# Two projection parts at a time by seven half-size products (Strassen's form) in a one-core decoder mixer layer

## The reference

```python
    h = _rmsnorm(x, g_pre) * (1 + scale[:, None]) + shift[:, None]
    p = h @ w_in
    hc, bc, cc, gc, q, k, v, ga = jnp.split(p, _split_points(), axis=-1)
    u = cc * hc
    conv_y = sum(conv_w[i] * u_pad[:, i:i + L] for i in range(CONV_WIDTH))
    ya = _rmsnorm(bc * conv_y, g_conv) * jax.nn.silu(gc)
    o = attend(q, k, v, b_sb).reshape(Bsz, L, ATT_DIM)
    yb = _rmsnorm(o, g_attn) * jax.nn.silu(ga)
    m = jnp.concatenate([ya, yb], axis=-1) @ w_out
    y = x + gate[:, None] * _rmsnorm(m, g_post)
```

## Time and profile before

| | |
|---|---|
| median of 3 runs | 873.62 us (872.91 to 875.14) |
| profiled execution, its own time | 872.5 us |
| its span in the trace | 870.7 us |
| PE busy | 825.4 us (95%) |
| DVE, POOL, ACT busy | 526.9, 376.9, 348.9 us |
| granted TensorE clock, mean | 0.989 of full speed |
| moved | 191 MB, 220 GB/s over the span |

### The profile page before, as it was taken

How to read it: one execution, slowest core, us unless ns; L and a number is a source line. 1 busy time by engine, 2 the same in 40 slices (tenths; PEclk the granted TensorE clock), 3 DMA queues, 4 the chain that set the end, 5 groups by cost and what they waited for, 6 DMA issues and landing times.

```text
span 870.7 us, 15500 instructions
## 1 busy us (share of the span) xinstructions
PE 825.4 (95%) x4267; PEld 488.4 (56%) x4267; DVE 526.9 (61%) x691; ACT 348.9 (40%) x682; POOL 376.9 (43%) x186
## 2 busy tenths in 40 slices
PE   0899989999999999999999999999999999899996
PEld 0455756555667565565765655658555555344442
DVE  2554678676584767737857768287686774223334
ACT  6311057574112575811136666211565741111222
POOL 0006782653677355525865455268446430100000
PEclk9989999999999999999999999999999999999998
DMA  8997685576788866657888675687986757373101
GB/s 320 331 309 254 219 268 168 170 226 207 234 253 270 276 208 215 222 172 252 270 271 261 223 244 177 200 256 252 282 249 212 238 185 302 106 236 100 71 24 51
DMA packets 129221, 191.25 MB, mean 220 GB/s; under 512 B 9817, under 2 KB 50822, under 8 KB 129121
## 3 DMA queue, kind: packets, MB, share of 16 engines
q1 hardware_dynamic: 97920, 174.38, 60.9%
q10 hardware_dynamic: 31200, 15.73, 6.4%
HBM read 181.58 MB, written 8.51 MB: 218 GB/s over the span
## 4 chain that ended last, share of the span: by engine, by line
PE 88%; DVE 3%; issue 2%; SPq 2%; DMA 2%; ACT 1%; POOL 1%; POOLq 0%; DVEq 0%; ACTq 0%
PE ps L1144 83%; PE ps L1300 4%; DMA pages<-in_page_table_dram 1%; PE ps L1185 1%; SPq L319 1%; POOL prod L539 1%; DMA hT<-in_w_out_dram 1%; DVE xy L851 1%; DVE ps L1024 0%; DMA ring<-in_cache_v_dram 0%; PE ps L1327 0%; SPq L359 0%; SPq L351 0%; DVE zc L1030 0%; ACT gcb L572 0%
## 5 line engine op out<-in xcount | busy, mean ns | idle before, releaser
L1144 PE MATMUL ps<-hT,wsl 128*128 128x344 f32 x1344 | 425.3, 458 | 3.5 <-issue 3.5
L539 POOL TENSOR_TENSOR prod<-ring,qb 128x1024 f32<-128x1024 f32 x128 | 313.2, 2470 | 220.3 <-DMA ring<-in_cache_k_dram 93.9
L1144 PEld LDWEIGHTS ps<-hT,wsl 128*128 128x128 f32 x1344 | 241.6, 190 | 156.7 <-issue 43.0
L1000 DVE TENSOR_REDUCE zd<-prod 128x16 f32<-128x1024 f32 x128 | 154.1, 1213 | 37.1 <-POOL prod L539 35.9
L1010 DVE TENSOR_SCALAR zc<-ps,bsb 128x512 f32<-128x512 f32 (+3 forms) x96 | 55.5, 613 | 70.3 <-PE ps L1144 68.9
L1144 PE MATMUL ps<-ring,apad 128*8 128x512 f32 (+1 forms) x608 | 82.9, 626 | 2.5 <-DMA ring<-in_cache_v_dram 2.2
L572 ACT ACTIVATE av<-ps 128x512 f32<-128x512 f32 (+3 forms) x96 | 46.7, 487 | 86.2 <-PE ps L1300 85.4
L1144 PE MATMUL ps<-hT,xy 128*128 128x512 f32 x160 | 72.1, 594 | 0.5 <-DMA hT<-in_w_out_dram 0.5
L1024 DVE TENSOR_TENSOR_SCAN ps<-rise,ps 128x512 f32<-128x512 f32 (+3 forms) x64 | 65.6, 1025 | 9.8 <-ACT ps L572 8.7
L1144 PEld LDWEIGHTS ps<-wsl,hT 128*128 128x128 f32 (+1 forms) x576 | 63.5, 181 | 6.2 <-ACT vN L572 2.6
L1144 PE MATMUL ps<-wsl,hT 128*128 128x128 f32 (+1 forms) x576 | 66.5, 275 | 0.0
(11 more groups left out here) (210 smaller groups left out, 662.6 us busy)
## 6 DMA issues: line engine op xcount, KB each, us to landing
ring<-in_cache_k_dram SPq DMA_DIRECT2D x256, 256.0 KB, 3.0
ring<-in_cache_v_dram SPq DMA_DIRECT2D x256, 256.0 KB, 3.0
wsl<-in_w_in_dram ACTq DMA_DIRECT2D x30, 512.0 KB, 5.7
ring<-in_w_ada_dram SPq DMA_DIRECT2D x6, 2048.0 KB, 11.3
xy<-in_x_prompt_dram SPq DMA_DIRECT2D x2, 2048.0 KB, 10.4
out_dram<-oT SPq DMA_DIRECT2D x8, 512.0 KB, 4.0
ring<-in_x_prompt_dram SPq DMA_DIRECT2D x8, 512.0 KB, 6.5
hT<-in_w_out_dram SPq DMA_DIRECT2D x5, 512.0 KB, 5.6
```

The lines of the kernel that those rows point to most:

```text
L539: pool.tensor_tensor(prod[:, p % 2].rearrange("p (j c) -> p j c", j=2), kring[:, p % 4], qb[:, p // 16].unsqueeze(1).to_broadcast([P, 2, H ...
L1000: v.tensor_reduce(zd[:, t // 16, :, r:r + 2], prod[:, t % 2].rearrange("p (j h d) -> p h j d", j=2, h=NH), AX_X, ALU.add)\
L1144: return nc.tensor.matmul(out, l, r, start=start, stop=stop, skip_group_check=True)
```

## The change

Two parts A (two blocks of 128 output channels) and the tokens B are cut in half along channels and tokens. Their product is made by seven products of half size in place of eight, in Winograd's form of Strassen's scheme. There are three pairs of parts (Q,K), (GC,GA), (HC,CC); in group 0 Q and K stay as they were, V and BC stay everywhere. So 11 pairs change.

- `channel_sums` on DVE makes T1 to T4, sums and differences of the quarters of `hT` (128x2064 each), once, in slot 0 of group 0, behind `gates(0)`. They take the room of `xy`, and more.
- `weight_sum` on POOL makes S1, S2, S4 and one sum in place (128x512 each) for each pair: 44 instructions. For (Q,K) of the next group they stand at the end of a group, for (GC,GA) in slots 7 and 8, for (HC,CC) in slots 17 to 20.
- `product(i, j)` on PE is half product `j` of half pair `i`: 4 matmuls with 258 moving tokens. Seven of them make 258 tokens of one half and 258 of the other, for both parts; two half pairs make a pair. They use three banks BX, BV, BY. ACT copies product 1 into BY (`st_seed`), so that BY can be added to, and copies out P5, U2 (`stage`), C11 and C21; DVE adds C12 and C22 (`product_sum`).
- Product 2 waits for `st_seed`, 3 for ACT's copy of P5, 7 for ACT's copy of U2, 4 for DVE's `product_sum(..., 7)`. In groups 1 to 3 the first of these sums stand in DVE's slots 3 and 6.
- The gated parts of groups 0 to 2 are written to DRAM (`y_parts`) in slot 6 of the next group and read back before the output projection (6 loads of 512 KB). The row `gp` goes the same way.
- `sp` has one buffer in place of two and `av` three in place of four. The silu steps on ACT and POOL are moved some slots later. `key_rows` uses the bank OB and stands a slot later. The decode sums use BX and BV.

```diff
-PJ = 24
+PJ = 6
...
-KS = ((range(0, 1), range(1, 2)), (range(2, 6), range(6, 8)))
+HB = NT // 2
+SC = HB // 2
+SLABS = ((0, 1), (0, 3), (1, 2))
+
+PIECES = {"open": (((0, 1, range(0, 2)),), ((0, 1, range(2, 4)),), ((0, 5, range(0, 2)),), ((0, 5, range(2, 4)),)),
+          "mid": (((0, 2, range(0, 1)),), ((0, 2, range(1, 2)),), ((0, 2, range(2, 4)), (0, 6, range(0, 2))), ((0, 6, range(2, 4)),)),
+          0: (((-1, 4, range(0, 1)),), ((-1, 4, range(1, 2)),), ((-1, 4, range(2, 4)), (0, 1, range(0, 4))), ((0, 5, range(0, 2)),)),
+          1: (((0, 5, range(2, 3)),), ((0, 5, range(3, 4)),), ((0, 2, range(0, 4)), (0, 6, range(0, 2))), ((0, 6, range(2, 4)),)),
+          2: (((0, 3, range(0, 1)),), ((0, 3, range(1, 2)),), ((0, 3, range(2, 4)), (0, 7, range(0, 2))), ((0, 7, range(2, 4)),))}
+
+EARLY = ((1, 5), (2, 6), (3, 7, 11), (4, 15), (12, 16), (13, 17))
...
+        T1, T2, T3, T4 = [xT4[:, 4 * HB * i:4 * HB * (i + 1)].rearrange("p (k c) -> p k c", k=4) for i in range(4)]
+        S1, S2, S4 = [wS[:, i, :].rearrange("p (k c) -> p k c", k=4) for i in range(3)]
...
+        BX, BV, BY = PJB, PJB + 1, MB
+        BANK = {1: BX, 2: BX, 5: BV, 3: BV, 6: BY, 7: BY, 4: BY}
...
@@ SP @@
+                    if not first and t == 6:
+                        for b, src in enumerate((gcb, gab)):
+                            sp_e.wait_ge(part_ready, 2 * g)
+                            sp_e.dma_start(y_parts[b][bass.ds(g - 1, 1)].rearrange("a p s -> (a p) s"), src[:, 0:SEQ])\
+                                .then_inc(part_out, 16)
...
+            sp_e.wait_ge(part_out, 32 * (GROUPS - 1))
+            sp_e.wait_ge(st_full[4], 6 * GROUPS - 2)
+            for k in range(GROUPS - 1):
+                for b in range(2):
+                    sp_e.dma_start(yT[:, GROUPS * b + k, :], y_parts[b, k]).then_inc(part_in, 16)
...
@@ POOL @@
+                    if t == 7:
+                        weight_sum(g, 1, 0)
+                        weight_sum(g, 1, 1)
+                    if t == 8:
+                        weight_sum(g, 1, 2)
+                        weight_sum(g, 1, 3)
+                    if t in (17, 18, 19, 20):
+                        weight_sum(g, 2, t - 17)
...
@@ ACT @@
-                    if t in (15, 25):
-                        silu_step(g, t // 25, 0)
-                    if t in (17, 27):
-                        silu_step(g, t // 27, 1)
-                        silu_step(g, t // 27, 2)
+                    if t in (21, 27):
+                        silu_step(g, t // 27, 0)
+                    if t in (23, 29):
+                        silu_step(g, t // 29, 1)
+                        silu_step(g, t // 29, 2)
...
@@ DVE @@
+            def channel_sums():
+                b11, b12 = hT[:, 0:4, 0:HB], hT[:, 0:4, HB:NT]
+                b21, b22 = hT[:, 4:8, 0:HB], hT[:, 4:8, HB:NT]
+                v.wait_ge(h_ready, 1 + 3 * KT)
+                v.tensor_tensor(T1, b12, b11, ALU.subtract).then_inc(t_sum, 1)
+                v.tensor_tensor(T3, b22, b12, ALU.subtract).then_inc(t_sum, 1)
+                v.wait_ge(t_sum, 2)
+                v.tensor_tensor(T2, b22, T1, ALU.subtract).then_inc(t_sum, 1)
+                v.wait_ge(t_sum, 3)
+                v.tensor_tensor(T4, b21, T2, ALU.subtract).then_inc(t_sum, 1)
...
+                    if not first and t in (3, 6):
+                        product_sum(g, first, t // 6, 3)
+                        product_sum(g, first, t // 6, 7)
+                    if u > 0 and u % 6 == 0:
+                        product_sum(g, first, 1 + u // 6, 3)
+                        product_sum(g, first, 1 + u // 6, 7)
...
                     if first and t in (0, 5):
                         gates(t // 5)
+                    if first and t == 0:
+                        channel_sums()
...
@@ PE @@
+                        if j == 2:
+                            pe.wait_ge(st_seed, n + 1)
...
+                        if j == 3:
+                            pe.wait_ge(e_p5, n + 1)
...
+                        if j == 7:
+                            pe.wait_ge(e_u2, n + 1)
+                        if j == 4:
+                            pe.wait_ge(d_c22, n + 1)
```

More of the change, by code:

```diff
@@ L96, in pairs_at, with pieces_at @@
     return (16 + late.index(slot),) if slot in late else ()
+def pieces_at(u):
+    i = u // 2
+    step, chunk = ("open", "mid")[i] if i < 2 else i % 3, 2 + i // 3
+    return [[(chunk + back, j, ks) for back, j, ks in piece] for piece in PIECES[step][2 * (u % 2):2 * (u % 2) + 2]]
 def quad_of(slot):
@@ L609, in _ @@
             act.wait_ge(qs_ps, 1)
[L610 removed]
+            run(qsP, ps[:, DB, :], ACT.Copy, qs_copied, scale=HD ** -0.5)
             act.wait_ge(qs_ps, 2)
@@ L640, in evac, with evac_v @@
+            def evac_v(g, first, c):
+                act.wait_ge(pj_full, PJ * g + c + 1)
+                src = ps[:, PJB + c % 2, :]
+                if c < 2:
+                    if c == 0 and not first:
                         act.wait_ge(vout, 16 * g)
-                    run(vN[:, 4 * (m - 6):4 * (m - 5), :], src.rearrange("p (t c) -> p t c", t=4), ACT.Copy, pj_free)
-                elif m == 8:
+                    run(vN[:, 4 * c:4 * (c + 1), :], src.rearrange("p (t c) -> p t c", t=4), ACT.Copy, pj_free)
+                else:
+                    load_w(g, CC_, 2)
@@ L713, in weights @@
                 act.wait_ge(lwT_full, NU * g + u + 1)
-                if not (first and u < 4):
-                    act.wait_ge(pv_done, NU * g + u - 3)
-                run(av[:, u % 4, 0:P * UNITS[u][2]], ps[:, Z + u % 3, 0:P * UNITS[u][2]], ACT.Exp, a_ready)
+                if not (first and u < 3):
+                    act.wait_ge(pv_done, NU * g + u - 2)
+                run(av[:, u % 3, 0:P * UNITS[u][2]], ps[:, Z + u % 3, 0:P * UNITS[u][2]], ACT.Exp, a_ready)
             def body(g, first, last):
@@ L745, in body @@
                     if t >= 8 and t < SLOTS and u % 2 == 1:
-                        evac(g, first, last, 9 + u // 2)
+                        i = u // 2
+                        for back, j in {0: ((-1, 4), (0, 1)), 1: ((0, 5), (0, 2), (0, 6)), 2: ()}[i % 3]:
+                            if i or not back:
+                                evac_st(g, first, last, 2 + i // 3 + back, j)
                     if first and t in (1, 5):
@@ L1040, in _ @@
             for step in range(6):
-                gating(GROUPS - 1, step)
+                gating(GROUPS - 1, step, True)
             links[0] = 0
```

431 lines of the change are left out of this document (321 added, 110 removed).

## The result

The changed kernel takes **897.02 us** (median of 4 runs, 895.36 to 898.62), the kernel before 873.31 beside it: 1.027 times as long (95% interval 1.024 to 1.029), 23.7 us slower. The forecast was 877.1 us with a range of 861 to 889.

A forecast was written before the change was run, and what follows sets the result against it. PE, busy 95% of the span, was taken to bound the kernel. 872.5 - 35.4 + 9.1 + 16.6 + 9.0 + 4.2 = 876.0 us profiled; the median is 1.1 higher, so 877.1 us, range 861 to 889.

The forecast's parts named there:

- Two times at which PE could reach product 4: Groups 2 and 3: PE could be at product 4 at 408.2 and 575.9, ahead of DVE's sums.
- the part of the forecast that was counted as slower: Forecast's own range, 869 to 885, had chance 0.48; just over half of it counted as slower, above 876.2.
- Fewer products, -35.4: PE's products: 56 matmuls of 444 ns replace 48 of 585 ns, 3.2 us less for each of 11 pairs, -35.4 us.
- rival C: PE's short matmuls don't keep pace: 490 ns a half product matmul and not 444, 905 us; chance 0.05.
- Group 0, +9.1: Channel sums in DVE's queue delay `gates(1)` and `turn(0)` by 8.2 us; 0.85 us of saving lost: +9.1 us.
- Product 4 waits for DVE, +16.6: Start of groups 1 to 3: PE waits 4.0, 5.8 and 6.8 us for DVE sums behind gating step 2, +16.6.
- rival B: DVE late a second time, at the second pair of product sums: 4.0 us in each of three groups, 889.1; chance 0.17.
- Attention units, +9.0: Between `scores` and `turn`, cover shrinks 0.85 us at units 0, 2, 4, 10, 16, 22; waits sum to +9.0 us.
- Rival A: At `turn` of units 0, 2, 16, 22 the units don't wait: 868.1 us without those 9.0; chance 0.30.
- POOL: "The others stand in slots where POOL has time", 0: POOL's weight sums, 1.3 us each, other than (Q,K)'s four: hidden where POOL has time, adding nothing.
- The clock, +4.2: After new PE waits a clock drop costs 1.7 us: half for group 1, one each for groups 2 and 3.
- Transfers, 0: Reading parts back from DRAM needs 11 us, covered by PE's work before the output projection: nothing, at most 2 us.

The follow-up runs named there:

- Runs 5: Changed kernel with DVE's four channel sums ahead of `gates(0)` in place of behind it: 885.92 us, 1.012 of the kernel before.
- 6: Kernel before with four additions of 128x2048 on DVE behind `gates(0)` in group 0, into a tile nobody reads: 882.76 us, 1.010.
- Run 7: Changed kernel with DVE's two product sums of the first half pair ahead of gating step 2 in place of behind it: 892.96 us, 1.021.
- run 12: Changed kernel with later reductions, early channel and product sums, spread read-back, and groups written out in place of the loop: 857.42 us, 0.982 of the kernel before.
- Runs 1: Changed kernel with POOL's (GC,GA) weight sums in slot 6 in groups 1 to 3, in slots 6, 9 and 10 in group 0: 884.31 us, 1.010.
- 2: Changed kernel with DVE's reductions of slots 9 to 31 one slot later, behind the next scan: 883.05 us, 1.009 of the kernel before.
- 3: Kernel before with four sums of 128x512 on POOL in slots 7 and 8 of each group, into a tile nobody reads: 883.28 us, 1.008.
- run 4: Changed kernel without the writes of the gated parts to DRAM and without their read-back: 886.61 us, 1.015 of the kernel before.

## Why the prediction was wrong

Its sum ran to 876.0 for the profiled execution; 898.6 came. The table of stretches splits the 22.6 us: 5 of work, 6 to 7 of idle, 11 of half clock. The sum itself is added up rightly. Two times at which PE could reach product 4 are 0.1 us too late (408.1 and 575.8), and the part of the forecast that was counted as slower, 0.23 of 0.48, is just under half of it and not just over.

- **Fewer products, -35.4: the work fell by 30.** The rival C (490 ns in place of 444) is false, but the price was a little low. Rows of half products with nothing between start 1.74 us apart, 435 ns a matmul, and 1.83 to 1.85 next to other work, as ahead of the last row here (after, group 3):

```profile
582.41 1.90 PE L1348 MATMUL ps<-xT,wS 128*128 128x258 f32 x8
584.15 1.90 PE L1348 MATMUL ps<-hT,wsl 128*128 128x258 f32 x8
585.89 1.90 PE L1348 MATMUL ps<-xT,wS 128*128 128x258 f32 x8
587.73 1.06 PE L1348 MATMUL ps<-ring,apad 128*8 128x512 f32 x8
```

  The cleanest measure is the pair of kernels written out: 165.9 and 157.9 us of work in a group with three pairs, so 2.7 us a pair and not 3.2. 144 matmuls of 585 ns less 8.0 us, over 168 matmuls, is 454 ns. The line through 128 and 344 columns gave 444 ns, 2% high for a steady row and 2% low for the mean. The mean has 42 short sequences a group in it, where there were 18; that their starts make the difference fits the 0.1 us at each, but no run shows it alone.
- **Group 0, +9.1: right.** The wait is 9.31 us, 8.5 more than before, and the sums take 2.3 us each (2.4 estimated). Runs 5 and 6 show the cause. The 2.08 us wait at `turn(0)` is one of 2.07 at `turn(1)` now. The text took the half clock behind the gates to be hidden, and it wasn't: from 110.4 to 115.0 the clock was 0.50 with PE busy throughout, 2.3 us, and a wait of 0.76 for POOL's first weight sum followed.
- **Product 4 waits for DVE, +16.6: right in kind and place, 13.2 in size.** 2.48, 3.82 + 1.10 and 5.78 against 4.0, 5.8 and 6.8. In group 2 product 2 waited for ACT first, as written, and inside the same 5 us. Run 7 shows the cause: step 2. Of that step's 4.9 us in group 3 the scan and the copy of two columns take 3.3, held by POOL's products (run 12), as they were before (3.7). The second pair of sums was waited for nowhere, so rival B didn't come.
- **Attention units, +9.0: mostly false.** Unit 22 waits 0.63, 0.63 and 0.47 us in groups 1 to 3, unit 16 about 0.2, unit 0 not at all: with units 1 and 6 some 3.9 us in the whole kernel, 0.6 before, `turn(2)` and group 0's `turn(1)` left aside, which belong to other terms. Rival A had this right. What is free at a unit can't be read off as the time from the subtraction to the transpose alone; once something upstream is late, DVE and ACT wait less for PE (this is argued; no run isolates it).
- **POOL: "The others stand in slots where POOL has time", 0. This is the step that failed.** Pair 17 came late behind the four sums of (GC,GA): 13.7 us at `turn(2)` in four groups, some 2 of it by the writes, and 8.1 us of half clock behind: together 21.8 us in this profile, where the miss is 22.6, and the other terms, some over and some under, come to about 1 us. Runs 1 and 2 give back 14 to 16 us of it, since other waits take a part of the place. The text took care of (Q,K)'s sums and of the tiles' due times, and called POOL's slots 7 and 8 free because POOL waits there. But POOL's waits in those slots are for keys and for DVE, and five microseconds of sums ahead of pair 17 aren't hidden by a wait that comes before pair 14. The prediction asked for the channel sums who stands behind them in the queue; asked here, the same question finds DVE's reduction of pair 17, which needs POOL's product, and behind it the scan of unit 2. Runs 1, 2 and 3 show it.
- **The clock, +4.2: 15.5.** Not the price of a drop (1.7 us for 3.4 us at half speed) was off but the number: seven stretches at 0.50 in the groups, where two and a half were priced, in two of them PE was busy 4.7 and 6.0 us and not 3.2 to 3.4, and one more in the output projection. A table of windows with PE busy behind the waits at `gate_sums(1)`, `turn(2)` (two rows) and `st_seed` (columns: window, length, PE, PEld, DVE, ACT, POOL busy, clock, DMA share, GB/s):

```profile
110.40:115.00 4.60, 4.60 (x16) 3.57 (x17) 3.17 (x4) 0.00 (x0) 3.07 (x2) 0.50 0.64 201
302.80:306.20 3.40, 3.40 (x12) 2.21 (x12) 0.90 (x2) 1.33 (x4) 2.35 (x1) 0.50 0.85 247
306.20:309.60 3.40, 3.40 (x25) 1.82 (x22) 2.61 (x4) 1.86 (x5) 0.00 (x0) 1.00 1.01 273
415.50:418.90 3.40, 3.40 (x8) 2.74 (x9) 3.40 (x3) 0.18 (x1) 3.31 (x2) 0.51 0.39 143
```

  The last row has 8 records, one half product, in 3.4 us; in the steady row above one takes 1.74.
- **Transfers, 0: false by 2 to 4 us.** Without the writes and the read-back the output projection is 3.6 us shorter, of which the w_out wait is 1.6 and a stretch of half clock 1.7, which may be chance (run 4). The estimate took the bandwidth and PE's 11.7 us of work, but the loads of `w_out` into `hT` can't start before PE has finished with `hT`, at 749.2 us, and the queues still moved 400 GB/s from 745 to 750 us in after, 9 GB/s at that place in run 4.

The bounds were drawn for each term that had been thought of. The change puts instructions ahead of paced ones on many queues, and the range had no room for one such place that was missed.

## What to carry to other kernels

Before calling an engine's time free, follow the next paced instruction behind the added work, across the engines: POOL's product, DVE's reduction, DVE's scan, PE's transpose. The added work is hidden only if it stands behind the last link that someone is waiting for; an in-order queue passes on lateness of work that PE doesn't need. When PE is bound at 95% and its work is cut by 4%, the cover of everything else shrinks with it, and each new wait of 3 to 4 us costs half as much again in clock. The other engines' order had to be written anew before the change was level with the kernel before, and with the loop written out in both it was worth 1.2%.
